# A gMLP stage inside a two-block transformer kernel: wide gate tiles with joined halves, mixing without slices, modulation units two by two

## What is computed

```python
def gmlp_mixer(h, w_in, ln_g, ln_b, ws, bs, w_out):
    B, S, _ = h.shape
    z = jax.nn.gelu(h @ w_in, approximate=False)
    u, v = z[..., :GM_HALF], z[..., GM_HALF:]
    v = layernorm(v, ln_g, ln_b)
    vc = v.reshape(B, S // GM_CHUNK, GM_CHUNK, GM_GROUPS, GM_GROUP_DIM)
    mixed = jnp.einsum('gpq,bnqgc->bnpgc', ws, vc) + bs.T[None, None, :, :, None]
    return (u * mixed.reshape(B, S, GM_HALF)) @ w_out
```

## Time and profile before

| | |
|---|---|
| median of 3 runs | 1231.38 us (1231.12 to 1231.49) |
| the profiled execution's own time | 1231.55 us |
| its span in the trace | 1229.8 us |
| PE busy | 1222.0 us, 99% of the span |
| DVE busy | 971.6 us, 79% |
| ACT busy | 703.5 us, 57% |
| PE clock granted | full in all 40 slices |

### The profile page before, as it was taken

How to read it: one execution, slowest core, us unless ns; L and a number is a source line. 1 busy time by engine, 2 the same in 40 slices (tenths; PEclk the granted TensorE clock), 3 DMA queues, 4 the chain that set the end, 5 groups by cost and what they waited for, 6 DMA issues and landing times.

```text
span 1229.8 us, 18608 instructions
## 1 busy us (share of the span) xinstructions
PE 1222.0 (99%) x7018; PEld 1063.2 (86%) x7018; DVE 971.6 (79%) x1234; ACT 703.5 (57%) x1061; POOL 125.8 (10%) x234
## 2 busy tenths in 40 slices
PE   9999999999999999999999999999999999999998
PEld 8989888888878988998999888888878998888887
DVE  5877999977976798898788778997784898676664
ACT  5555555657575555555777556555654253755552
POOL 2000000010011211111133101120010010000000
PEclk9999999999999999999999999999999999999999
DMA  9756777666553798893232358997565597385550
GB/s 305 251 163 213 244 246 235 227 207 187 192 170 103 246 334 309 314 334 116 74 106 71 135 181 291 392 392 247 187 212 200 172 318 264 118 292 191 186 187 35
DMA packets 154840, 265.80 MB, mean 216 GB/s; under 512 B 6108, under 2 KB 110675, under 8 KB 154774
## 3 DMA queue, kind: packets, MB, share of 16 engines
q1 hardware_dynamic: 136246, 205.29, 49.4%
q0 software_dynamic: 18352, 59.54, 14.0%
q10 hardware_dynamic: 176, 0.07, 0.0%
HBM read 263.79 MB, written 1.09 MB: 215 GB/s over the span
## 4 chain that ended last, share of the span: by engine, by line
PE 93%; DVE 4%; ACT 1%; POOL 1%; issue 0%; POOLq 0%; ACTq 0%
PE ps L2078 24%; PE ps L2058 18%; PE ps L2061 9%; PE ps L2042 4%; PE ps L2044 4%; PE ps L2043 4%; PE ps L2099 2%; PE ps L2101 2%; PE ps L2100 2%; PE ps L2121 2%; PE ps L2123 2%; PE ps L2122 2%; PE ps L2487 2%; DVE w_lo L1218 1%; PE ps L2178 1%; PE ps L2180 1%
## 5 line engine op out<-in xcount | busy, mean ns | idle before, releaser
L1218 DVE TENSOR_TENSOR w_lo<-raw,w_hi 128x2048 fp32r<-128x2048 f32 (+3 forms) x211 | 434.0, 2071 | 32.3 <-ACT w_hi L615 32.0
L615 ACT ACTIVATE w_hi<-raw 128x2048 fp32r<-128x2048 f32 (+3 forms) x213 | 368.6, 1737 | 51.2 <-PE ps L2078 43.5
L2058 PE MATMUL ps<-xn,w_hi 128*128 128x512 f32 x976 | 243.8, 392 | 0.0
L2058 PEld LDWEIGHTS ps<-xn,w_hi 128*128 128x128 f32 x976 | 178.2, 188 | 34.3 <-issue 0.4
L2061 PEld LDWEIGHTS ps<-xn,w_lo 128*128 128x128 f32 x976 | 133.1, 190 | 9.5
L2061 PE MATMUL ps<-xn,w_lo 128*128 128x256 f32 x976 | 136.1, 282 | 0.0
L2078 PE MATMUL ps<-w_hi,a_hi 128*128 128x512 f32 x432 | 134.6, 393 | 0.0
L695 ACT ACTIVATE work<-ps 128x512 f32<-128x512 f32 x61 | 36.3, 595 | 170.0 <-PE ps L2061 170.0
L2078 PE MATMUL ps<-w_lo,a_hi 128*128 128x512 f32 x432 | 133.5, 390 | 0.0
L2078 PE MATMUL ps<-w_hi,a_lo 128*128 128x512 f32 x432 | 133.2, 389 | 0.0
L2042 PE MATMUL ps<-xn,w_hi 128*128 128x256 f32 x432 | 122.8, 284 | 0.0
(11 more groups left out here) (378 smaller groups left out, 2004.0 us busy)
## 6 DMA issues: line engine op xcount, KB each, us to landing
raw<-in_ffn_w SPq DMA_DIRECT2D x64, 1024.0 KB, 5.5
side<-in_ada_w POOLq DMA_DIRECT2D x96, 512.0 KB, 6.2
raw<-in_ffn_w_in SPq DMA_DIRECT2D x40, 1024.0 KB, 5.2
raw<-in_ffn_w_out SPq DMA_DIRECT2D x32, 512.0 KB, 5.0
raw<-in_gm_w_in SPq DMA_DIRECT2D x16, 1024.0 KB, 6.1
raw<-in_od_w_in SPq DMA_DIRECT2D x12, 1024.0 KB, 5.9
raw<-in_gm_w_out SPq DMA_DIRECT2D x8, 1024.0 KB, 5.7
raw<-in_ev_w_in SPq DMA_DIRECT2D x6, 1024.0 KB, 13.0
```

The lines of the kernel that those rows point to most:

```text
L615: nc.scalar.activation(w_hi[s][:, 0:w], raw[s][:, 0:w], ACT.Copy).then_inc(hi_done, 1)
L1218: nc.vector.tensor_tensor(w_lo[s][:, 0:w], raw[s][:, 0:w], w_hi[s][:, 0:w].bitcast(F32), ALU.subtract)\
L2058: nc.tensor.matmul(o, hi, xn[:, 512 * k:512 * k + 512], start=k == 0, stop=False)
```

## The change

It touches the gMLP stage only.

- The gate tiles are computed by `f_wide`, into banks 0 and 1, tile 1 alone into banks 6 and 7. ACT copies the right halves out, DVE joins, and ACT applies Gelu to the joined values in SBUF.
- In ACT's program the copy of tile j is followed by the split, and only then by the wait for the join and the Gelu.
- In DVE's program the join of step j stands behind the bias add of step j (from step 2 on); join 0 stands between the two splits ahead of step 0, join 1 behind the product of step 0.
- On PE `gm_u(j)`, from j = 3 on, waits for the join of step j - 1 (tile 2 for the join of step 0), since it takes the same banks.
- The mixing matmuls read `gm_v` where it is, and the eight slices go; the mixing waits for the norm's quarter instead. Three waits of DVE for its own norm instructions go too.
- The eight modulation units are spread over steps 3 to 6, two in each.

```diff
-        J_RELU1 = J_RELU0 + R_STEPS - 2
+        J_GM = J_RELU0 + R_STEPS - 2
+        J_RELU1 = J_GM + GM_STEPS
...
+        def gm_u_bank(j):
+
+            return 6 if j == 1 else 0
...
-            gm_u = wk(6144, 512)
+            gm_u = [wk(6144 + 512 * m, 512) for m in (1, 0)]
...
+            def gm_low(j):
+
+                act.wait_ge(w_used, T_GM + f_at(j, GM_STEPS) + 1)
+                low_copy(gm_u[j % 2], gm_u_bank(j))
 
             def gm_step(j):
                 f, par = T_GM + f_at(j, GM_STEPS), j % 2
-                act.wait_ge(w_used, f + 1)
-                nc.scalar.activation(gm_u, ps[par][:, :], ACT.Gelu).then_inc(GM["u"], 1)
+                if j != 1:
+                    gm_low(j)
                 if 2 <= j < GM_STEPS - 1:
                     split(f + 4)
+                act.wait_ge(join_done, J_GM + j + 1)
+                nc.scalar.activation(gm_u[par], gm_u[par], ACT.Gelu).then_inc(GM["u"], 1)
+                if j == 0:
+                    gm_low(1)
                 act.wait_ge(GM["prod"], j + 1)
...
                 for t in range(TT):
                     last = nc.vector.scalar_tensor_tensor(vv[t], vv[t], rstd[:, 36 + t:37 + t], shift, ALU.mult, ALU.add)
-                if q % 2:
-                    last.then_inc(side_used, 1)
-                    dve.wait_ge(side_used, units[1] + 1)
-                else:
-                    chain(last)
+                    if t == 0 or q % 2 == 0:
+                        last.then_inc(GM["vs"], 1)
+                    else:
+                        last.then_inc(side_used, 1)
...
-            def gm_slice(j):
-
-                return nc.vector.tensor_copy(gm_vs, gm_v[:, :, j * 256:j * 256 + 256]).then_inc(GM["vs"], 1)
+            def gm_join(j):
+
+                join(gm_u[j % 2], gm_u_bank(j), J_GM + j + 1)
...
                     .then_inc(GM["t"], 1)
-                if j + 1 < GM_STEPS:
-                    gm_slice(j + 1)
+                if j >= 2:
+                    gm_join(j)
                 if 2 <= j < GM_STEPS - 1 and j != 3:
                     split(f + 4)
                 dve.wait_ge(GM["t"], j + 1)
                 dve.wait_ge(GM["u"], j + 1)
-                nc.vector.tensor_tensor(gm_t[par], gm_t[par], gm_u, ALU.mult).then_inc(GM["prod"], 1)
+                nc.vector.tensor_tensor(gm_t[par], gm_t[par], gm_u[par], ALU.mult).then_inc(GM["prod"], 1)
+                if j == 0:
+                    gm_join(1)
                 if j == 3:
                     split(f + 4)
...
-                if 3 <= j < 6:
-                    for kb in range(3 * j - 9, min(3 * j - 6, KB)):
+                if 3 <= j < 7:
+                    for kb in range(2 * j - 6, 2 * j - 4):
...
-            gm_slice(0)
             split(T_GM + 2)
+            gm_join(0)
             split(T_GM + 3)
...
             def gm_u(j):
                 if j >= 2:
-                    pe.wait_ge(GM["u"], j - 1)
-                f_tile(T_GM + f_at(j, GM_STEPS), j % 2)
+                    pe.wait_ge(join_done, J_GM + (1 if j == 2 else j))
+                f_wide(T_GM + f_at(j, GM_STEPS), gm_u_bank(j))
 
             def gm_mix(j):
 
-                pe.wait_ge(GM["vs"], j + 1)
+                pe.wait_ge(GM["vs"], (2, 3, 5, 6)[j // 2])
+                if j // 2 % 2:
+                    pe.wait_ge(side_used, U_BC2 + 2 * (j // 4) + 2)
                 if j >= 2:
                     pe.wait_ge(GM["t"], j - 1)
                 for b in range(2):
                     for t in range(TT):
                         c = (2 * b + t) * P
-                        last = nc.tensor.matmul(ps[2 + j % 2][:, c:c + P], gm_vs[:, t, b * P:b * P + P],
+                        last = nc.tensor.matmul(ps[2 + j % 2][:, c:c + P], gm_v[:, t, 256 * j + b * P:256 * j + b * P + P],
                                                 gm_wst[:, j * P:j * P + P], start=True, stop=True)
...
             gm_u(0)
+            pe.wait_ge(GM["v"], 6)
             gm_u(1)
             gm_mix(0)
             gm_u(2)
             gm_mix(1)
+            pe.wait_ge(join_done, J_GM + 2)
             gm_t_step(0)
```

More of the change, by code:

```diff
@@ L1194, in build @@
         gm_bs, gm_wst, gm_ws = wk(4096, 1024), wk(5120, 1024), wk(6144, 1024)
-        gm_u = wk(6144, 512)
+        gm_u = [wk(6144 + 512 * m, 512) for m in (1, 0)]
         gm_t = [acc[:, 4, 512 * m:512 * m + 512] for m in range(2)]
-        gm_vs = acc[:, 3, 0:512].rearrange("p (t c) -> p t c", t=TT)
         SEG = [(0, P), (P, 3 * P)]
```

## The result

| | before | changed |
|---|---|---|
| median | 1231.38 us (1231.00 to 1231.59, 7 runs) | 1235.67 us (1235.36 to 1235.86, 7 runs) |
| profiled execution, its span | 1231.55, 1229.8 us | 1235.75, 1234.0 us |
| forecast | | 1236.0, range 1233.6 to 1237.8 |

The account below looks back on a forecast made before the run. PE was taken as the bound, with DVE close behind. -1.5 us for the tiles, +4.9 for three stalls and +1.2 at the boundary gave +4.6, so a median of 1236.0 us, range 1233.6 to 1237.8.

Parts of the forecast that it names:

- The gate tiles: gMLP stage on PE: a wide tile takes 5.56 us instead of 5.75, saving 0.19 on each of 8 tiles, 1.5 us.
- The rule on matmuls: Gate tiles: columns at 2.4 GHz plus about 2.5 ns would save only 0.04 us a tile, result 1236.9; not used.
- What DVE gains and loses: DVE's queue: eight slices of 0.33 us go, eight joins of 0.61 come, +0.28 a step; the join's place matters.
- Tiles 3 and 4: PE waits for joins 2 and 3: tile 3 starts at 979.95, tile 4 at 993.8; stalls 1.3 and 1.9 us.
- Tiles 5 and 6: PE doesn't wait: an output product of 5.6 us lies between, bias add and join need 1.2.
- Tile 7: Built-in wait for join 6, whose bias add needs mixing 6: 1.75 us; tile 7 starts at 1025.8.
- The boundary: Before relu1: follows DVE's queue, first residual at 1043.6 (+4.7), 1.2 us beyond the tail's 3.45; PE room at most 0.2.
- Behind it: relu1, after the boundary: runs PE-bound as relu0 did, and hides or returns nothing.
- the first two: Rivals: joins always in time at tiles 3 and 4, 1229.9, chance 0.05; only tile 7's stall real, 1231.6, chance 0.12.
- The one with more room at the boundary: Rival: the stalls are there, but the boundary has more room than read; +3.4 us, 1234.8, chance 0.15.
- The dearer passages between engines: Rival: copy, join, Gelu, product passages at 0.35 instead of 0.12 us; +1.5 us in all, 1237.5, chance 0.1.
- the units: Two by two in steps 3 to 6: DVE stands 1.5 us before bias add 6; step 6 carries 2.54 us more.

Follow-up runs that it names:

- e6: Changed kernel with joins 2 and 3 moved early and gate tiles 6 and 7 narrow, units two by two; +0.12 us against the kernel before, ratio 1.0001.
- e7: Changed kernel with joins 2 and 3 early, tiles 6 and 7 narrow, units two, three, three in steps 3 to 5; -1.07 us against the kernel before, ratio 0.9992.
- e11: Repeat: changed kernel with joins 2 and 3 early, tiles 6 and 7 narrow, units two, three, three; -1.34 us against the kernel before, ratio 0.9990.
- e4: Changed kernel with joins 2 and 3, and ACT's copies for them, moved to earlier places; +1.18 us against the kernel before, ratio 1.0006.
- e3: Changed kernel with each join from step 2 on ahead of the bias add instead of behind it; +3.09 us against the kernel before, ratio 1.0023.
- e5: Changed kernel with gate tiles 6 and 7 alone narrow, in a bank each, without their copies and joins; +3.11 us against the kernel before, ratio 1.0026.
- e1: Changed kernel with all gate tiles narrow again, no copies or joins; direct reads and units two by two stay; +1.10 us against the kernel before, ratio 1.0007.
- e8: Changed kernel with the old units (three, three, two in steps 3 to 5); +5.96 us against the kernel before, ratio 1.0046; profiled execution +4.8 us.
- e2: Changed kernel with narrow gate tiles and old units (three, three, two), only the direct reads left; 0.00 us against the kernel before, ratio 0.9999.
- e10: Repeat of the changed kernel with the old units (three, three, two in steps 3 to 5); +5.95 us against the kernel before, ratio 1.0047.
- e9: Wide gate tiles alone: changed kernel with slices, DVE's three norm waits and old units back; +8.50 us against the kernel before, ratio 1.0076; profiled execution +7.0 us.

## Why the prediction was right

It was 0.3 us off (1236.0 against 1235.67). The mechanism is the one that it named: three waits of PE for joins, at tiles 3, 4 and 7, and a boundary that follows DVE. Its steps can be held against the traces one by one. The first four of these lines are from the changed kernel, the last three from the kernel before:

```profile
948.41 1.98 PE L2072 MATMUL ps<-xn,w_hi 128*128 128x512 f32 x8
953.97 2.00 PE L2072 MATMUL ps<-xn,w_hi 128*128 128x512 f32 x8
...
960.36 1.87 PE L2072 MATMUL ps<-xn,w_hi 128*128 128x512 f32 x7
...
966.04 1.06 PE L2809 MATMUL ps<-work 128*128 128x128 f32 x8
```

```profile
948.39 0.28 PE L2042 MATMUL ps<-xn,w_hi 128*128 128x256 f32 x1
...
991.41 0.28 PE L2042 MATMUL ps<-xn,w_hi 128*128 128x256 f32 x1
...
1028.08 1.06 PE L2793 MATMUL ps<-work,acc 128*128 128x128 f32 x8
```

- *The gate tiles*: 5.56 us forecast. Tile 0 starts at 948.41 and tile 1 at 953.97: 5.56. But the forecast is right only for tiles that follow an output product or each other. Tile 2, behind a mixing, takes 5.68, and tiles 3, 4 and 7, behind their waits, take 5.71, 5.70 and 5.70. The narrow tile takes 5.75 behind an output product and 5.83 behind a mixing (1022.25 to 1028.08).
- *The rule on matmuls*: The Trainium skill's rule for the gap between matmuls (TensorE: Matmul & The Clock Gate, section Back-to-back issue gap), which it gives for an isolated matmul, would have left a saving of 0.04 us a tile. The traces don't agree: matmuls of 512 columns start 0.23 us apart (rule: 0.216) and those of 256 columns 0.12 us (rule: 0.109). By the rule six wide tiles save 0.2 us; e6, e7 and e11, which have six and no wait in the steps, save 1.1 us up to the tail.
- *What DVE gains and loses*: bias add 2 forecast at 978.55, found at 978.52; bias add 3 at 992.4, found at 992.29.
- *Tiles 3 and 4*: forecast at 979.95 and 993.8, found at 979.85 and 993.62. e4 shows the cause: with the two joins elsewhere both waits are gone. *Tiles 5 and 6*: no wait, as forecast. (The place of tile 4 before, 991.4, is right, but the rows named for it give 998.22 - 0.82 - 5.75 = 991.65; the timeline has 991.41.)
- *Tile 7*: forecast at 1025.8, found at 1025.64. e3 and e5 show that it comes from the join standing behind the bias add and from the banks shared with tile 6. Three small terms make up the 0.2 us: mixing 6 ends at 1024.01 and not at 1024.08, DVE follows it 0.28 us later and not 0.35, and the restart takes 0.13 us (from 979.72, the join's end by the next instruction, to tile 3 at 979.85; the same at tile 7) and not 0.2.
- *The boundary*: first residual forecast at 1043.6, found at 1043.53, +4.65. But the transposes are at 1048.59, +4.2 and not +4.6. **The room there was mis-sized.** The prediction gave PE "at most 0.2 us of room". PE needs only the first half of the scaled rows: where it waits for them, it starts 0.54 us behind the start of the scaling (1048.59 - 1048.05; 0.55 in e1 and e6), so before it could have started at 1043.94, and it came at 1044.39. The room was 0.45. The prediction's own rows left 0.55 (the half was done at 1043.84), less about 0.1 for the restart.
- *Behind it*: the first matmul of relu1 is at 1051.08, against 1046.83 before, +4.25, and the span ends 4.2 later. Nothing was hidden or given back.

The sum itself hit better than its terms. From tile 0 to mixing 7 PE takes 82.93 us instead of 79.69, 3.24 more, and the stalls between starts are 4.4. So the tiles gave 1.2 us and not 1.5, the stalls cost 4.4 and not 4.9, and the boundary took 0.9 (4.2 - 3.24) and not 1.2. The first two errors nearly cancel, and that is luck; the third is the room.

Of the rivals, the first two fall with the waits at tiles 3 and 4 (the first was also priced too near: by the prediction's own numbers it needed 1.25 us more room at bias add 2, but 1.9 at bias add 3). The one with more room at the boundary was right in direction and a third in size, or less. The dearer passages between engines fall with the restart of 0.13 us, and with step 3: its product starts 1.45 us behind its join (994.34 - 992.89), of which the join and the Gelu fill 0.68 and 0.63, so that two passages have 0.14.

Of the units the prediction said that DVE would stand 1.5 us ahead of bias add 6; it stands 1.40. It put no price on their spread. The experiments do: spread over four steps they spare 0.5 us in front of tile 7 (1.38 against 1.86 in e8's profiled run) and 0.4 at the first residual, and without the wide tiles they cost 1.1 us (e1 against e2).

## What to carry to other kernels

When an accumulation needs a second engine before its bank is free again, what counts, here at least, is less that engine's work than the place of the freeing instruction in its queue. Put it as soon as its input is there, ahead of anything that depends on later work of the engine that waits. Here the same instructions in another order (e4) took a loss of 4.3 us down to 1.2. The step from there to a gain of 1.1 to 1.3 (e7, e11) needed more than order: tiles 6 and 7 in the narrow form, since the order tried there (e3) only shortened the wait, and the units out of step 6. And work moved out of one queue's crowded stretch should be checked against the next point where that queue is late: the units spared the steps and hit the boundary.

## What was not expected of the hardware

Single runs of the same kernel are longer by one step of about 1.2 us. One of them was profiled: e11's profiled execution took 1231.02 us where its other runs took 1229.6 to 1230.0. Set beside e7's, the same kernel, its timeline of PE has, from 20 us on, one wait that the other lacks, and it lies 380 us ahead of the gMLP stage, at the end of the second gated feed-forward:

```profile
566.85 1.97 PE L2162 MATMUL ps<-cst,work 128*128 128x128 f32 x16 [0.80 <-DVE work L1510]
```

In e7 these matmuls start at 565.65. The cause lies another 116 us back, in a split of ACT that waited for its weight load:

```profile
450.75 1.92 ACT L620 ACTIVATE w_hi<-raw 128x2048 fp32r<-128x2048 f32 x1 [1.57 <-DMA raw<-in_ffn_w_in]
```

In e7 the same split starts at 449.14 and waits for nothing. From there on most of what ACT and DVE do is 1.2 to 1.4 us late (a later activation at 513.30, against 511.89), but PE is not: the copies behind its tiles start at 459.29 and 543.22, against 459.34 and 543.27. Only where PE needs DVE's last product of the feed-forward does the delay reach it, and then it stays. So in this run the step has nothing to do with the change. Why that load came late is open.

In e8, e10 and e9 most runs had such a step or two, in the other kernels none or one. Whether it is the same one, met more often, isn't settled: the profiled executions of these three kernels were all among the short runs. In e8 and e9 the long runs list a lower mean granted clock (0.998 and 0.997, against 1.000), and these kernels have PE's longest waits (1.9 and 2.9 us); in e10, with e8's kernel, the clock doesn't separate the long runs from the short ones. Where in a long run the clock was lower no trace shows. The expectations of these runs hold for their profiled executions (+4.8 and +7.0) and not for their medians.
